# Expert outputs brought home in pairs shifted by one, combining groups in twos, row transposes split, attention halves alternating

## What is computed

```python
h = modulate(rmsnorm(x, g_mix), sh1, sc1)
qa, ka, va, qb, kb, vb, rb, lg = project_inputs(h, w_in, w_gate_up, b_gate)
oa = swa_sample(qa, ka, va, past_k, past_v, sinks)     # or swa_prompt
s_new, ob = gla_block(past_s.astype(jnp.float32), qb, kb, vb, lg)
x = x + gt1 * mixer_output(oa, ob, rb, g_head, w_out)
h = modulate(rmsnorm(x, g_ffn), sh2, sc2)
x = x + gt2 * moe_ffn(h, w_rg, b_rg, w_re, b_re, w_eg, w_eu, w_ed)
# attention: 16 query heads of 64, 2 key heads; a sample has 128 cached keys and 16 new ones
s = jnp.einsum('btjgd,bsjd->bjgts', q, k) * (SWA_HEAD_DIM ** -0.5)
p = softmax_with_sink(s, sink)
o = jnp.einsum('bjgts,bsjd->btjgd', p, v)
# experts: 32, each token goes to 2; each expert has three matrices of 4 MB
return (jax.nn.silu(xblk @ w_eg[e]) * (xblk @ w_eu[e])) @ w_ed[e]
```

## Time and profile before

| what | value |
|---|---|
| median of 3 runs | 1809.2 us (1808.55 to 1809.29) |
| the profiled execution | 1807.56 us, its span 1806.0 us |
| TensorE busy | 1694.2 us, 94% of the span |
| VectorE busy | 686.5 us, 38% |
| ScalarE busy | 191.7 us, 11% |
| memory read and written | 596.21 MB and 11.62 MB, 337 GB/s over the span |
| the chain that ended last | PE 78%, DMA 16%, DVE 4% |
| up, L1256 | 4096 records, 471.7 us |
| down, L1281 | 1024 records, 226.8 us |
| combining, L1297 | 768 records, 193.0 us |

### The profile page before, as it was taken

The page is one execution under the profiler, slowest core; times in us unless marked ns, Lnnn a source line. Parts: engine busy times, 40 slices in busy tenths (PEclk is TensorE's granted clock), DMA queues, the critical chain, the costliest instruction groups (busy, mean ns, idle before and its releaser), DMA issues.

```text
span 1806.0 us, 23612 instructions
## 1 busy us (share of the span) xinstructions
PE 1694.2 (94%) x9621; PEld 856.2 (47%) x9621; DVE 686.5 (38%) x1355; ACT 191.7 (11%) x518; POOL 118.2 (7%) x263
## 2 busy tenths in 40 slices
PE   5999999999999999979999999999999999999993
PEld 2455454444455444456445544454445444544441
DVE  2012222225232230353543455345534553455376
ACT  3001111111211100111000000000000000000002
POOL 1031000000100130021000000000000000000000
PEclk9999999999999999989999999999999999999997
DMA  9998777665722586459999999999999999999981
GB/s 364 386 318 299 299 280 295 237 261 212 261 64 83 163 240 167 163 240 380 426 428 426 429 426 428 428 427 427 428 426 426 426 428 426 426 425 429 425 357 71
DMA packets 96632, 598.14 MB, mean 331 GB/s; under 512 B 12609, under 2 KB 14769, under 8 KB 61753
## 3 DMA queue, kind: packets, MB, share of 16 engines
q1 hardware_dynamic: 85106, 565.43, 77.1%
q0 software_dynamic: 11472, 31.95, 6.1%
HBM read 596.21 MB, written 11.62 MB: 337 GB/s over the span
## 4 chain that ended last, share of the span: by engine, by line
PE 78%; DMA 16%; DVE 4%; issue 1%; ACT 1%; SPq 0%; DVEq 0%; ACTq 0%; POOL 0%; POOLq 0%
PE bank L1256 18%; DMA ring<-in_w_expert_gate 14%; PE bank L1297 10%; PE bank L819 9%; PE bank L1281 8%; PE bank L1119 7%; PE bank L815 7%; PE bank L773 3%; PE bank L760 2%; PE bank L1146 2%; PE bank L739 2%; DMA ring<-in_w_ada 1%; PE bank L1239 1%; PE bank L764 1%; PE bank L1057 0%
## 5 line engine op out<-in xcount | busy, mean ns | idle before, releaser
L1256 PE MATMUL bank<-ring,zbuf 128*64 128x256 f32 x4096 | 471.7, 383 | 17.7 <-DMA ring<-in_w_expert_gate 16.9
L1256 PEld LDWEIGHTS bank<-ring,zbuf 128*64 128x64 f32 x4096 | 290.4, 137 | 238.1 <-issue 86.1
L1281 PE MATMUL bank<-ring,hbuf 128*64 128x512 f32 x1024 | 226.8, 595 | 24.0 <-ACT hbuf L1637 24.0
L1297 PE MATMUL bank<-zbuf,modr 64*128 64x512 f32 x768 | 193.0, 616 | 6.3 <-DVE stat L2267 3.3
L819 PE MATMUL bank<-ring,hbuf 128*128 128x512 f32 x384 | 174.2, 599 | 2.9 <-ACT xbuf L1416 2.6
L2199 DVE TENSOR_TENSOR hbuf<-bank,dbuf 128x512 f32<-128x512 f32 x192 | 123.5, 685 | 97.6 <-PE bank L1297 95.8
L1281 PEld LDWEIGHTS bank<-ring,hbuf 128*64 128x64 f32 x1024 | 72.8, 137 | 155.9 <-issue 150.2
L815 PE MATMUL bank<-hbuf,ring 128*128 128x384 f32 x384 | 133.8, 495 | 1.2 <-ACT zbuf L1412 0.8
L1119 PE MATMUL bank<-ring,zbuf 128*128 128x512 f32 x288 | 127.0, 596 | 3.1 <-DVE ring L1940 1.9
L2204 DVE TENSOR_TENSOR xbuf<-xbuf,hbuf 128x512 f32<-128x512 f32 x192 | 124.1, 688 | 3.3
L819 PEld LDWEIGHTS bank<-ring,hbuf 128*128 128x128 f32 x384 | 70.2, 190 | 83.6 <-issue 82.6
(11 more groups left out here) (395 smaller groups left out, 1207.7 us busy)
## 6 DMA issues: line engine op xcount, KB each, us to landing
ring<-in_w_expert_up SPq DMA_DIRECT2D x64, 2048.0 KB, 18.9
ring<-in_w_expert_gate SPq DMA_DIRECT2D x64, 2048.0 KB, 21.1
ring<-in_w_expert_down SPq DMA_DIRECT2D x64, 2048.0 KB, 18.9
ring<-in_w_ada SPq DMA_DIRECT2D x96, 1024.0 KB, 8.3
ring<-in_w_in SPq DMA_DIRECT2D x32, 1024.0 KB, 9.5
ring<-in_w_out SPq DMA_DIRECT2D x16, 1024.0 KB, 5.1
xbuf<-in_x_prompt SPq DMA_DIRECT2D x4, 1024.0 KB, 6.0
xbuf<-in_x_sample SPq DMA_DIRECT2D x2, 1024.0 KB, 8.2
```

Of the source, the lines that this page charges most:

```text
L1256: last = mm(bank[2 + j // 4][64 * q:64 * q + 64, 0:256], xeT[u][:, k % 8, k // 8, :], w[:, kk_, 256 * q:256 * q + 256], start=(k == 0), st ...
L1281: last = mm(bank[5 + n][64 * q:64 * q + 64, :], hidT[u][:, k % 2, k // 2, :], unit(8 + k)[:, 1024 * q + QN * n:1024 * q + QN * n + QN], st ...
L1297: return mm(bank[b][:, :], hot[u][r, t * P:t * P + P], ysb[u][r, QN * (n % 2):QN * (n % 2) + QN], start=start, stop=stop)
```

## The change

There are four edits.

1. **Pairs shifted by one.** A pass now covers experts e - 2 and e - 1 and is laid into `up` of the odd expert e, so the pairs are (1, 2), (3, 4), up to (29, 30). Expert 0 is alone in `up` of expert 1. Even experts have no pass. VectorE's `add_group` and `expert_gates` move with it; for expert 31 `expert_gates` now comes before the copy of y.
2. **Groups in twos.** Two groups are issued together, after units 1, 3 and 5, no longer one after each of units 0 to 5.
3. **Row transposes split.** Four of the next expert's eight row transposes come before `hidden_T`, four after it. ScalarE copies the activations first and its half of the rows second; VectorE's half waits for the first four alone (`eT_first`).
4. **Attention halves alternating.** Products of the two halves alternate. In the sample values all products with cached keys come first and all with new keys second.

```diff
@@ -854,20 +854,20 @@
                 if s == 16:
                     pe.wait_ge(qs_sb, 1)
                     pe.wait_ge(past_sb, 4)
-                for u in range(2):
-                    out = bank[4 + u]
-                    r = slice(64 * u, 64 * u + 64)
-                    if s < 16:
-                        t, m = STEPS[s]
-                        nk = P * (t + 1)
-                        last = mm(out[:, 0:nk], zT[r, m, t * P:(t + 1) * P], kT2[r, m // 4, 0:nk], start=True, stop=True)
-                    else:
-                        b = s - 16
-                        for j in range(SWA_KV):
-                            q = q_s[r, b, j, :]
-                            mm(out[r, 144 * j:144 * j + 128], q, past_kT[r, b, j, :], start=True, stop=True)
-                            last = mm(out[r, 144 * j + 128:144 * j + 144], q, kT2[r, j, 256 + 16 * b:272 + 16 * b],
-                                      start=True, stop=True)
+                rows = (slice(0, 64), slice(64, 128))
+                if s < 16:
+                    t, m = STEPS[s]
+                    nk = P * (t + 1)
+                    for u, r in enumerate(rows):
+                        last = mm(bank[4 + u][:, 0:nk], zT[r, m, t * P:(t + 1) * P], kT2[r, m // 4, 0:nk], start=True, stop=True)
+                else:
+                    b = s - 16
+                    for j in range(SWA_KV):
+                        for u, r in enumerate(rows):
+                            mm(bank[4 + u][r, 144 * j:144 * j + 128], q_s[r, b, j, :], past_kT[r, b, j, :], start=True, stop=True)
+                        for u, r in enumerate(rows):
+                            last = mm(bank[4 + u][r, 144 * j + 128:144 * j + 144], q_s[r, b, j, :],
+                                      kT2[r, j, 256 + 16 * b:272 + 16 * b], start=True, stop=True)
                 last.then_inc(sc_ps, 1)
 
             def probs_T(s):
@@ -898,21 +898,25 @@
                 if s == 16:
                     pe.wait_ge(vnew_in, 16)
                 out = bank[4][:, 384:512]
-                for u in range(2):
-                    r = slice(64 * u, 64 * u + 64)
-                    if s < 16:
-                        t, m = STEPS[s]
-                        j = m // 4
-                        for kt in range(t + 1):
+                rows = (slice(0, 64), slice(64, 128))
+                if s < 16:
+                    t, m = STEPS[s]
+                    j = m // 4
+                    for kt in range(t + 1):
+                        for u, r in enumerate(rows):
                             last = mm(out[r, 0:P], kva[:, kt, 128 + 64 * j:192 + 64 * j],
                                       PT[:, s % 2, (2 * u + kt) * P:(2 * u + kt + 1) * P], start=(kt == 0), stop=(kt == t))
-                    else:
-                        b = s - 16
-                        for j in range(SWA_KV):
+                else:
+                    b = s - 16
+                    for j in range(SWA_KV):
+                        for u, r in enumerate(rows):
                             mm(out[r, 64 * j:64 * j + 64], cache_v[:, b, 64 * j:64 * j + 64],
-                               PT[:, s % 2, j * P + 64 * u:j * P + 64 * u + 64], start=True, stop=False)
+                               PT[:, s % 2, j * P + 64 * u:j * P + 64 * u + 64], start=(j == 0), stop=False, skip_group_check=True)
+                    for j in range(SWA_KV):
+                        for u, r in enumerate(rows):
                             last = mm(out[r, 64 * j:64 * j + 64], v_new[:, b, 64 * j:64 * j + 64],
-                                      PT[0:16, s % 2, 256 + j * P + 64 * u:256 + j * P + 64 * u + 64], start=False, stop=True)
+                                      PT[0:16, s % 2, 256 + j * P + 64 * u:256 + j * P + 64 * u + 64], start=False, stop=(j == 1),
+                                      skip_group_check=True)
                 last.then_inc(o_ps, 1)
 
             for n in range(20):
@@ -1232,12 +1236,19 @@
                 last = mm(bank[6][:, 0:NE], ones[:, :], rt[:, ORDER[j], 96:128], start=(j == 0), stop=(j == NT - 1))
             last.then_inc(table_ps, 1)
 
-            def rows_T(u, e, gat_need):
+            def rows_T(u, h, signal):
+
+                rows = xg[u].rearrange("p (n c) -> p c n", c=8)
+                for c in range(4):
+                    last = tr(bank[h][:, c * P:(c + 1) * P], rows[:, 4 * h + c, :], ident[:, :])
+                last.then_inc(signal, 1)
+
+            def rows_first(u, gat_need):
                 pe.wait_ge(gat[u], gat_need)
-                rows = xg[u].rearrange("p (n c) -> p c n", c=8)
-                for c in range(8):
-                    last = tr(bank[c // 4][:, (c % 4) * P:(c % 4 + 1) * P], rows[:, c, :], ident[:, :])
-                last.then_inc(eT_ps, 1)
+                rows_T(u, 0, eT_first)
+
+            def rows_second(u):
+                rows_T(u, 1, eT_ps)
 
             def expert_landed(j, e):
                 j -= j % 2
@@ -1257,7 +1268,8 @@
                                       xeT[u][:, k % 8, k // 8, :], w[:, kk_, 256 * q:256 * q + 256],
                                       start=(k == 0), stop=(k == KC - 1))
                     last.then_inc(unit_used, 1)
-                    if between and j < 6:
+                    if between and j % 2 and j < 6:
+                        between(j - 1)
                         between(j)
 
             def hidden_T(u, e):
@@ -1297,7 +1309,7 @@
                 return mm(bank[b][:, :], hot[u][r, t * P:t * P + P], ysb[u][r, QN * (n % 2):QN * (n % 2) + QN],
                           start=start, stop=stop)
 
-            def combine(g, before, rows):
+            def combine(g, before, rows, us):
 
                 if g == 0:
                     pe.wait_ge(hot_rdy, rows)
@@ -1305,28 +1317,29 @@
                     pe.wait_ge(y_a, rows)
                 if g >= 2:
                     pe.wait_ge(comb_x, before + g - 1)
-                us = (0,) if isinstance(rows, int) and rows == NE - 1 else (0, 1)
                 for u in us:
                     for q in range(2):
-                        last = back_to_tokens(g // 2, 2 * q + g % 2, GROUP_BANKS[g % 2][q], u, u == 0, u == us[-1])
+                        last = back_to_tokens(g // 2, 2 * q + g % 2, GROUP_BANKS[g % 2][q], u, u == us[0], u == 0)
                 last.then_inc(comb_ps, 1)
 
-            rows_T(0, 0, 16)
+            rows_first(0, 16)
+            rows_second(0)
 
             def two_experts(i):
                 for u in range(2):
                     e = 2 * i + u
                     if isinstance(i, int) and e == 1:
                         pe.wait_ge(gates_sb, 1)
-                    if isinstance(i, int) and e == NE - 1:
-                        up(u, e, e + 1, lambda g: combine(g, 6 * (NE // 2 - 1), NE - 1))
-                    elif u == 0 and not (isinstance(i, int) and i == 0):
-                        up(u, e, e + 1, lambda g: combine(g, 6 * (i - 1), 2 * i))
+                    if u:
+                        up(u, e, e + 1, lambda g: combine(g, 6 * i, e, (0,) if isinstance(i, int) and i == 0 else (1, 0)))
                     else:
                         up(u, e, e + 1)
-                    if not (isinstance(i, int) and e == NE - 1):
-                        rows_T(1 - u, e + 1, 16 * i + 16 * (1 + u))
+                    last = isinstance(i, int) and e == NE - 1
+                    if not last:
+                        rows_first(1 - u, 16 * i + 16 * (1 + u))
                     hidden_T(u, e)
+                    if not last:
+                        rows_second(1 - u)
                     if isinstance(i, int) and e == 0:
                         gate_rows()
                     down(u, e)
@@ -1344,7 +1357,8 @@
                             if t + n:
                                 pe.wait_ge(over_x, 12 * i + 4 * t + n)
                             back_to_tokens(t, n, 7).then_inc(over_ps, 1)
-                    rows_T(0, e, 16 * 17 + 16 * i)
+                    rows_first(0, 16 * 17 + 16 * i)
+                    rows_second(0)
                     up(0, e, e + 1)
                     hidden_T(0, e)
                     down(0, e, i + NE)
@@ -1641,8 +1655,8 @@
                     e = 2 * i + u
                     exp_gate(u, e)
                     if isinstance(i, int) and e == 0:
+                        hidden_copy(u, e)
                         rows_copy(1 - u, e + 1)
-                        hidden_copy(u, e)
                         for q, b in ((0, 3), (1, 7)):
                             act.wait_ge(rows_ps, q + 1)
                             last = cp(gate_row[:, TOK * q:TOK * q + TOK], bank[b][:, 128:512])
@@ -2107,7 +2121,7 @@
             cp(stat[:, 43:44], stat[:, 0:1]).then_inc(dest_rdy, 1)
 
             def rows_copy(u, n):
-                dve.wait_ge(eT_ps, n + 1)
+                dve.wait_ge(eT_first, n + 1)
```

(20 more changed lines are left out.)

2 lines of the change are left out of this document (1 added, 1 removed).

## The result

| | before | after |
|---|---|---|
| median of the runs | 1808.88 us (1808.30 to 1809.29, 4 runs) | 1789.86 us (1789.47 to 1793.05, 4 runs) |
| ratio | | 0.9899, 95% interval 0.9882 to 0.9916 |
| profiled execution, its span | 1807.56, 1806.0 us | 1789.56, 1787.8 us |

The forecast was 1793.6 with a range of 1789 to 1802; the median lies within 1 us of the range's lower end. In the kernel after, `up` is L1267, combining L1309, row transposes L1243, `hidden_T` L1279, `down` L1293.

The account below looks back on a forecast made before the run. TensorE was taken to bound attention, weight transfers the expert loop, TensorE and VectorE the tail. Attention 11.3, tail 2.6 and last gates 1.7 sum to 15.6 us less: 1809.2 to 1793.6 us, range 1789 to 1802.

Parts of the forecast that it names:

- Sample scores: Attention, 8 steps: alternating halves needs two slots of 0.36 us instead of three, 2.9 us less.
- Sample values: Attention, 8 steps: two runs of eight records replace eight runs of two, 1.05 us less a step, 8.4 in all.
- Rival (a): Attention: halves do not overlap on shared rows; only 8.9 us less in all, 1800.3; chance 0.10.
- Rival (c): Attention: the edit does nothing there, softmax latency or an eviction being next; 4.3 us less, 1804.9; chance 0.06.
- Prompt steps: Attention, 16 steps of prompt scores and values: already overlapping in the old order, taken as zero.
- Expert loop: Expert pairs: TensorE needs about 57 us a pair, but transfers take 60.07 and cover the gain; worth 0.
- Tail: Behind the last weight wait: full combining moves to expert 31, whose down starts at 1761.6 against 1764.22; 2.6 us less.
- TensorE follows the transfers to the first unit of 31: 1704.58 + 30.03: Tail: expert 30 has no combining, so the first unit of 31 comes at 1734.61.
- Rival (b): Tail: attention as forecast, but the tail worth nothing through a late add or late last weight; 1797.9; chance 0.06.
- last gates: Kernel end: VectorE builds the last selection rows before the copy of y, while waiting for down; 1.7 us less.
- Last selections: Kernel end: the last selection rows, built before the copy of y instead of after it; 1.7 us less.
- if the granted clock leaves 1.00 between 850 and 1750 us: Expert part: a sign in TensorE's clock that would show the forecast wrong.
- Rival (d): Even experts: waits for weights halve TensorE's clock, 19 us lost per such pair; decides from 61.1 us a pair; chance 0.03.

Follow-up runs that it names:

- halves alone: Kernel before with the attention edit only, its sample values alternating halves but not grouped by shape; median 1798.54 us, ratio 0.9942 to before.

## Why the prediction was right

The forecast for the profiled execution was 15.6 us less. The span fell by 18.2.

**Sample scores**, forecast 2.9: 2.8, eight times 0.353.

**Sample values**, forecast 8.4: 10.1. The mechanism was right, the size off. The term that was mis-sized is the run of eight records, taken as 0.47 us "by the step and the change above": it takes 0.38. I stepped by 0.11 each time, the distance of the first record to the second in the earlier trace rows; the later ones follow at 0.059 and 0.058. So 0.107 + 0.059 + 0.058 and 0.151 for the change of shape make 0.375. The 0.15 for a change was right: two runs more per step cost 0.3 us (halves alone). A step had eight runs, with seven changes between them and one ahead of the first; "eight turns have become one" counts one too many.

Rival (a) is out. Its run of 0.92 us was mis-sized by the same step: by the distances above, halves in single file would have taken 0.107 + 6 x 0.058 + 0.151 = 0.61 us. The rule that a weight load overlaps running products only when the row group differs (the Trainium skill, TensorE: Matmul & The Clock Gate, "What overlaps and what doesn't") gives by the same working 0.61 us a run. Products on all 128 rows and on two column halves took 0.38. Rival (c) is out by the landmark.

**On the way to the experts** 12.9 us became 11.5. The first sample scores came 0.9 us later than in before, and so did the first prompt scores (160.87 against 159.96 us), where no edit reaches. In after the clock had stood at half for 3.4 us at 44 us, in before not; the three profiles without such a fall reach the first sample scores at 342.3 to 342.5 us, the eleven with one at 342.8 to 344.3. A second fall, at 641 us, cost after 1.6 us of its lead. The kernel before had one of the same length at 776 us, and that one gave 1.7 back. The last 0.6 went in the wait for the gathered rows of expert 0, before and after:

```profile
813.13 1.97 PE L1239 MATMUL bank<-ident,zbuf 128*128 128x128 f32 x8 [6.58 <-DMA zbuf<-h_rows,cur]
801.61 1.97 PE L1243 MATMUL bank<-ident,zbuf 128*128 128x128 f32 x8 [7.20 <-DMA zbuf<-h_rows,cur]
```

**Prompt steps**, forecast 0: from the first prompt scores to the first sample scores it is 182.33 us with the edit and 182.34 without.

**Expert loop**, forecast 0: the DMA share stays 1.01 and pairs 60.1 us, with the edits and without them. TensorE's own pair of 56.50 us is close to the forecast's 57. The way there was not quite the forecast's: in the kernel before TensorE also waited 0.77 us for the gates ahead of the first group of a pair (at 867.32 us), which the sum left out, and the new place of the transposes gave 0.3 us in one expert of a pair and 0.6 in the other, where 0.6 in each was forecast.

**Tail**, forecast 2.6. The part from the first unit of 31 to down is exact (26.99 against 26.98). The start of 31 is not: 1720.94, where 1734.61 - 11.52 = 1723.1 was due. The step that failed is "TensorE follows the transfers to the first unit of 31: 1704.58 + 30.03". The 30.03 is an average of two unlike experts. A transfer of 2 MB lands 4.89 us behind the one ahead of it, so six make 29.4 us. For each gather of rows that runs beside them, the transfers take some 0.66 us more (one of 5.55, or 5.38 and 5.08). In the second half of the loop both gathers of a pair fall into the same expert's transfers, so the first weights of successive experts land 30.7 and 29.4 us apart by turns, 60.1 a pair. In the kernel before the last gather landed at 1683.7 us, and the first weights of 31 at 1733.79, 29.35 behind those of 30: its trace had the answer, 0.7 us less than the 30.03. In after the last gather landed at 1663.3, no slower transfer follows, and the last pair of experts takes 58.85 us (1662.09 to 1720.94). The other 1.5 us are the stream's own: the first transfer of expert 1 landed 13.91 us behind the first unit against 15.07 in before, and 0.4 came along the way. Neither is the edits' doing as far as the runs show, for that first transfer landed between 13.8 and 16.7 us in the profiles, with and without them. These 1.5 us are luck.

Rival (b) is out: of the tail, undoing each part gave 1.9 us for the selections, 1.9 for the shift and about 1 for the groups and transposes. Its 1797.9 also left out the last gates, which a late add or weight would not have touched; with them it is 1796.2.

**Last selections**, forecast 1.7: 1.9, by undoing it.

Sum of what was measured: 11.5 to the first unit, 2.15 of earlier start of 31, 2.6 of the tail as worked out, 1.9 behind down's start = 18.15 of 18.2. The stretches follow each other without a gap, so they must add up; the causes rest on the experiments. By landings: 13.0 up to the last one and 5.2 behind it. Of the 5.2, 1.9 are the last selections, 1.9 the shift and 1.0 the groups and transposes, each by undoing it; 0.4 is left over.

So the forecast's 15.6 against 18.2 is the sum of errors both ways: the values gave 1.7 more and the start of 31 2.15 more, and 1.4 was lost on the way to the experts, most of it where no edit reaches.

**Clock**: the sign "if the granted clock leaves 1.00 between 850 and 1750 us" came, from 853 to 860 us, and yet the forecast held. In expert 1 TensorE waited 2.58 us for VectorE, then the clock stood at half for 6.8 us and down took 9.45 instead of 7.09. It cost nothing that can be seen: the DMA share stayed 1.01, and from 1000.62 us on TensorE waited for transfers. Rival (d) needs pairs above 61.1 us; the clock fell once, not in every even expert.
